# A streaming encoder layer on one Trainium2 core: the first prompt tile routed by quarters of its heads

## The reference

```python
def peer_block(xb, w_pq, sub_keys, u_tab, v_tab):
    q = (xb @ w_pq).reshape(T, PEER_HEADS, 2, D_HALF)
    s = jnp.einsum('thcd,ckd->thck', q, sub_keys)
    s1, i1 = lax.top_k(s[:, :, 0], PEER_TOPK)
    s2, i2 = lax.top_k(s[:, :, 1], PEER_TOPK)
    cand = (s1[..., :, None] + s2[..., None, :]).reshape(T, PEER_HEADS, PEER_TOPK * PEER_TOPK)
    cidx = (i1[..., :, None] * N_KEYS + i2[..., None, :]).reshape(T, PEER_HEADS, PEER_TOPK * PEER_TOPK)
    best, sel = lax.top_k(cand, PEER_TOPK)
    eidx = jnp.take_along_axis(cidx, sel, axis=-1)
    g = jax.nn.softmax(best, axis=-1)
    u = jnp.take(u_tab, eidx, axis=0)
    a = jax.nn.gelu(jnp.einsum('thkd,td->thk', u, xb).astype(jnp.float32))
    vv = jnp.take(v_tab, eidx, axis=0)
    return jnp.einsum('thk,thkd->td', (g * a).astype(xb.dtype), vv)
```

## Time and profile before

| what | value |
|---|---|
| three runs | 2685.37, 2688.01, 2691.91 us, median 2688.01 |
| the profiled execution | 2683.65 us, of which its span is 2682.1 us |
| mean granted PE clock | 0.971 |
| busy share of the span | PE 93%, PEld 83%, DVE 67%, POOL 40%, ACT 35% |
| memory traffic | 723.70 MB, mean 270 GB/s |

### The profile page before, as it was taken

The page is one execution under the profiler, slowest core; times in us unless marked ns, Lnnn a source line. Parts: engine busy times, 40 slices in busy tenths (PEclk is TensorE's granted clock), DMA queues, the critical chain, the costliest instruction groups (busy, mean ns, idle before and its releaser), DMA issues.

```text
span 2682.1 us, 41611 instructions
## 1 busy us (share of the span) xinstructions
PE 2483.2 (93%) x15886; PEld 2232.5 (83%) x15886; DVE 1793.9 (67%) x2208; ACT 941.4 (35%) x1146; POOL 1069.9 (40%) x615
## 2 busy tenths in 40 slices
PE   5989899999799999698888899999999999999998
PEld 4878777788799999698888899899888777787777
DVE  4555654543465666586756665667589889898898
ACT  3354544522323333222222222233333333333332
POOL 1020101020000037778878888842145444444442
PEclk8999999999899999899999999999999999999999
DMA  5453544495234556798889999998799999999997
GB/s 183 133 181 111 180 127 137 143 393 171 81 111 143 158 159 159 202 308 285 292 287 293 294 307 300 301 342 357 270 395 412 412 413 412 412 412 413 410 412 284
DMA packets 221593, 723.70 MB, mean 270 GB/s; under 512 B 55656, under 2 KB 105576, under 8 KB 154823
## 3 DMA queue, kind: packets, MB, share of 16 engines
q1 hardware_dynamic: 132304, 397.46, 41.6%
q0 software_dynamic: 86976, 315.74, 33.1%
q10 hardware_dynamic: 2231, 9.44, 0.9%
HBM read 680.73 MB, written 41.83 MB: 269 GB/s over the span
## 4 chain that ended last, share of the span: by engine, by line
PE 36%; POOL 22%; DMA 18%; DVE 13%; issue 7%; ACT 1%; SPq 1%; DVEq 1%; ACTq 0%; POOLq 0%
POOL g_dense L473 18%; PE banks L1208 10%; PE banks L1210 10%; PE banks L1209 10%; DMA a_tile<-a_dense 6%; DVE h L1160 5%; DMA raw<-in_v_tab 4%; POOL u_row L467 4%; DMA g_dense<-route,route_place 3%; PE banks L1434 2%; DMA v_raw<-in_v_tab 2%; DVE v_lo L1168 2%; DMA raw<-in_w_out 1%; DVE ring_lo L1168 1%; DVE ring_lo L808 1%
## 5 line engine op out<-in xcount | busy, mean ns | idle before, releaser
L1208 PE MATMUL banks<-xT_hi,ring_hi 128*128 128x256 f32 (+1 forms) x2304 | 698.9, 303 | 92.9 <-DVE ring_lo L1057 88.1
L473 POOL DMA_INDIRECT g_dense<-route,route_place x256 | 503.0, 1965 | 488.8 <-DVE route_place L1116 371.3
L1209 PE MATMUL banks<-xT_lo,ring_hi 128*128 128x256 f32 (+1 forms) x2304 | 672.1, 292 | 0.0
L1210 PE MATMUL banks<-xT_hi,ring_lo 128*128 128x256 f32 (+1 forms) x2304 | 672.0, 292 | 0.0
L1208 PEld LDWEIGHTS banks<-xT_hi,ring_hi 128*128 128x128 f32 x2304 | 448.9, 195 | 98.9 <-DVE ring_lo L1057 93.9
L501 POOL DMA_INDIRECT v_row<-in_v_tab,route_place x128 | 338.4, 2644 | 418.0 <-DVE h L1160 367.7
L1057 DVE TENSOR_TENSOR ring_lo<-banks,ring_hi 128x1024 fp32r<-128x1024 f32 x256 | 309.8, 1221 | 209.3 <-ACT ring_hi L732 208.0
L1209 PEld LDWEIGHTS banks<-xT_lo,ring_hi 128*128 128x128 f32 x2304 | 448.9, 195 | 0.0
L1210 PEld LDWEIGHTS banks<-xT_hi,ring_lo 128*128 128x128 f32 x2304 | 447.4, 194 | 0.0
L732 ACT ACTIVATE ring_hi<-banks 128x1024 fp32r<-128x1024 f32 x256 | 262.5, 1026 | 520.8 <-PE banks L1434 519.4
L1124 DVE CUSTOM_DVE_ANT_0 u_row<-u_row,x_rows 128x2048 f32<-128x2048 f32 x128 | 291.8, 2287 | 168.9 <-DMA u_row<-in_u_tab,route_place 168.0
(11 more groups left out here) (216 smaller groups left out, 3802.0 us busy)
## 6 DMA issues: line engine op xcount, KB each, us to landing
raw<-in_u_tab SPq DMA_DIRECT2D x128, 1024.0 KB, 5.9
v_raw<-in_v_tab SPq DMA_DIRECT2D x64, 1024.0 KB, 14.7
raw<-in_v_tab SPq DMA_DIRECT2D x64, 1024.0 KB, 14.3
raw<-in_w_in SPq DMA_DIRECT2D x160, 256.0 KB, 3.5
raw<-in_w_out SPq DMA_DIRECT2D x64, 256.0 KB, 4.3
g_dense<-zeros POOLq DMA_DIRECT2D x16, 1024.0 KB, 27.6
raw<-in_w_pq SPq DMA_DIRECT2D x64, 256.0 KB, 3.7
a_dense<-gelu_out SPq DMA_DIRECT2D x128, 128.0 KB, 5.9
```

The costliest lines, as they stand in the source:

```text
L473: pool.indirect_dma_start(out=places, out_offset=bass.IndirectOffsetOnAxis(ap=routeU[:, t, 2, j:j + 1], axis=0), in_=route[:, t, 0, j:j + ...
L1208: MM(out, h1, h2, start=first, stop=False)
L1209: MM(out, h1, l2, start=False, stop=False)
L1210: return MM(out, l1, h2, start=False, stop=last)
```

## The change

- Tile 0 is routed by `routing_quarter(nb, j)`: two heads at a time, in 6 parts, with buffers of its own (`cand4`, `eq4`). Quarter 0 has its parts behind steps 8, 9 and 12 of the query projection, quarter 1 behind step 13 and m = 0 to 3, quarter 2 in m = 4 to 8, quarter 3 in m = 8 to 12. Each quarter has its own exponential on ACT and its own count in `rt_ready`.
- The sample tile is routed in m = 13 to 25, tile 1 in every second m from 26 to 50. Dots are spread over m = 26 to 124, 1.306 a step.
- POOL scatters tile 0 as its quarters come. The sample rows' gathers begin at slot 104 of tile 0, one behind every two scatters; behind tile 0 POOL gathers alone, up to row 36; then it waits for tile 1 and sends two gathers with every three scatters.

```diff
-TILE_ORDER = (0, 2, 1)
-FIRST, SECOND = N_SWEEPS + N_PARTS, N_SWEEPS + 2 * N_PARTS
+QUARTERS = 4
+QUARTER_IN_PQ = {8: ((0, 0),), 9: ((0, 1), (0, 2), (0, 3)), 12: ((0, 4), (0, 5)), 13: ((1, 0), (1, 1))}
+QUARTER_IN_U = {0: ((1, 2),), 1: ((1, 3),), 2: ((1, 4),), 3: ((1, 5),), 4: ((2, 0),), 5: ((2, 1),), 6: ((2, 2), (2, 3)),
+                7: ((2, 4),), 8: ((2, 5), (3, 0)), 9: ((3, 1),), 10: ((3, 2), (3, 3)), 11: ((3, 4),), 12: ((3, 5),)}
+ROUTED = QUARTERS + NT - 1
+SAMPLES = 13
+DOTS_FROM = SAMPLES + N_PARTS
-AHEAD_ROWS = 48
+APART = 104
...
-            sp.wait_ge(rt_ready, NT)
+            sp.wait_ge(rt_ready, ROUTED)
...
-            for n in range(N_SCATTER // 2):
-                t, j = divmod(2 * n, SLOTS)
...
+            for j in range(SLOTS):
+                if j % (2 * TOPK) == 0:
+                    pool.wait_ge(rt_ready, 1 + j // (2 * TOPK))
+                if j % TOPK == 0 and j:
+                    pool.wait_ge(g_scat, 16 * j)
+                scatter(0, j)
+                if j == APART:
+                    pool.wait_ge(rt_ready, QUARTERS + 1)
+                if j >= APART and j % 2 == 0:
                     gather_dot(gathered)
                     gathered += 1
+            while gathered < dots_after(DOTS_FROM + 2 * N_PARTS) + NUB - 1:
+                gather_dot(gathered)
+                gathered += 1
+            pool.wait_ge(rt_ready, ROUTED)
+            for j in range(SLOTS):
+                if gathered < DOTS and j % 3 < 2:
+                    gather_dot(gathered)
+                    gathered += 1
+                if j % TOPK == 0:
+                    pool.wait_ge(g_scat, 16 * (SLOTS + j))
+                scatter(1, j)
...
+            few = [P, 2, TOPK, TOPK]
+
+            def routing_quarter(nb, j):
+
+                heads, places, pair = slice(2 * nb, 2 * nb + 2), slice(32 * nb, 32 * nb + 32), (2 * nb, 2 * nb + 1)
+                k = slice(0, 8) if j == 0 else slice(8, 16)
+                if j == 0:
+                    V.tensor_copy(tf[:, 4 * nb:4 * nb + 4, :], ti[:, 0, 4 * nb:4 * nb + 4, :])
+                    V.tensor_tensor(cand4[:, :, :].rearrange("p h (a b) -> p h a b", a=TOPK),
+                                    tvh[:, 0, heads, 0, :].unsqueeze(3).broadcast_to(few),
+                                    tvh[:, 0, heads, 1:2, :].broadcast_to(few), ALU.add)
+                    drain()
+                elif j == 1:
+                    for i, h in enumerate(pair):
+                        V.match_replace(cand4[:, i, :], bv[:, h, 0:8], cand4[:, i, :], NEG)
+                    drain()
+                if j < 2:
+                    for i, h in enumerate(pair):
+                        V.max(bv[:, h, k], cand4[:, i, :])
+                    drain()
+                    for i, h in enumerate(pair):
+                        V.max_index(bi[:, h, k], bv[:, h, k], cand4[:, i, :])
+                elif j == 2:
+                    V.tensor_copy(bst[:, 0, heads], bv[:, heads, 0])
+                    V.tensor_scalar(bhl[:, 0, heads], bi[:, heads, :], 4, None, ALU.logical_shift_right)
+                    V.tensor_scalar(bhl[:, 1, heads], bi[:, heads, :], 15, None, ALU.bitwise_and)
+                    drain()
+                    V.tensor_tensor(bv[:, heads, :], bv[:, heads, :], bst[:, 0, heads].unsqueeze(2).broadcast_to([P, 2, TOPK]),
+                                    ALU.subtract).then_inc(best_rdy, 1)
+                    V.tensor_copy(bhf[:, :, heads, :], bhl[:, :, heads, :])
+                elif j < 5:
+                    c = j - 3
+                    V.tensor_tensor(eq4[:, :, :, :], bhf[:, c, heads].unsqueeze(3).broadcast_to(few),
+                                    cst[:, C_IOTA:C_IOTA + 16].unsqueeze(1).unsqueeze(1).broadcast_to(few), ALU.is_equal)
+                    drain()
+                    V.tensor_tensor(eq4[:, :, :, :], eq4[:, :, :, :], tfh[:, heads, c:c + 1, :].broadcast_to(few), ALU.mult)
+                    drain()
+                    V.tensor_reduce(route[:, 0:1, 1 + c, places].rearrange("p o (h k) -> p (o h) k", h=2), eq4[:, :, :, :], AX.X, ALU.add)
+                else:
+                    dve.wait_ge(best_exp, nb + 1)
+                    V.tensor_reduce(bst[:, 0, heads], bv[:, heads, :], AX.X, ALU.add)
+                    drain()
+                    V.reciprocal(bst[:, 1, heads], bst[:, 0, heads])
+                    drain()
+                    V.tensor_tensor(route[:, 0:1, 0, places].rearrange("p o (h k) -> p (o h) k", h=2), bv[:, heads, :],
+                                    bst[:, 1, heads].unsqueeze(2).broadcast_to([P, 2, TOPK]), ALU.mult)
+                    i1 = route[:, 0:1, 1, places].rearrange("p o x -> p (o x)")
+                    i2 = route[:, 0:1, 2, places].rearrange("p o x -> p (o x)")
+                    place = bhf[:, 0, heads, :].rearrange("p h k -> p (h k)")
+                    V.scalar_tensor_tensor(out=place, in0=i2, scalar=float(P), in1=i1, op0=ALU.mult, op1=ALU.add)
+                    drain()
+                    V.tensor_scalar(routeU[:, 0:1, 2, places].rearrange("p o x -> p (o x)"), place, cst[:, C_AD + NT:C_AD + NT + 1],
+                                    cst[:, C_AD:C_AD + 1], ALU.mult, ALU.add).then_inc(rt_ready, 1)
+                drain()
+
...
+                for quarter, part in QUARTER_IN_PQ.get(s, ()):
+                    routing_quarter(quarter, part)
...
+                for quarter, part in QUARTER_IN_U.get(m, ()):
+                    routing_quarter(quarter, part)
                 if tile_part(m):
-                    n, j = tile_part(m)
-                    routing_part(TILE_ORDER[n], j)
+                    routing_part(*tile_part(m))
```

More of the change, by code:

```diff
@@ L57 @@
 UR = 4
-AHEAD_ROWS = 48
+APART = 104
 def tile_part(m):
[L63 to L66, removed]
+    if SAMPLES <= m < DOTS_FROM:
+        return NT - 1, m - SAMPLES
+    i = m - DOTS_FROM
+    return (1, i // 2) if i >= 0 and i % 2 == 0 and i < 2 * N_PARTS else None
 def dots_after(m):
-    return min(DOTS, max(m + 1 - SECOND, 0) * DOTS // (LAST_DOT - SECOND))
+    return min(DOTS, max(m + 1 - DOTS_FROM, 0) * DOTS // (LAST_DOT - DOTS_FROM))
 TD = SEQ
@@ L208, in hybrid_layer @@
         cand = at("cand", WK + 32, [P, PH, 256])
+        cand4 = at("cand_quarter", WK + 44, [P, 2, 256])
+        eq4 = at("eq_quarter", WK + 46, [P, 2, TOPK, TOPK])
         eqb = at("eq", WK + 40, [P, PH, TOPK, TOPK])
@@ L503, in gather_row @@
                     in_offset=bass.IndirectOffsetOnAxis(ap=routeU[:, NT - 1, 1, k:k + 1], axis=0)).then_inc(row_in[k % NVB], 16)
-            pool.wait_ge(rt_ready, NT)
             pool.wait_ge(dot_done, DOTS)
@@ L724, in _, with best_weights @@
                     score_evac(s // 4 - 1)
+                for quarter, part in QUARTER_IN_PQ.get(s - 1, ()):
+                    if part == 2:
+                        act.wait_ge(best_rdy, quarter + 1)
+                        A(bv[:, 2 * quarter:2 * quarter + 2, :], bv[:, 2 * quarter:2 * quarter + 2, :], ACT.Exp).then_inc(best_exp, 1)
+            def best_weights(n, heads):
+                act.wait_ge(best_rdy, n + 1)
+                A(bv[:, heads, :], bv[:, heads, :], ACT.Exp).then_inc(best_exp, 1)
             def u_hi(m, k):
@@ L749, in _ @@
                     A(adot[:, :], adot[:, :], ACT.Gelu_apprx_tanh).then_inc(dot_gelu, 1)
-                if m and tile_part(m - 1) and tile_part(m - 1)[1] == 6:
-                    act.wait_ge(best_rdy, tile_part(m - 1)[0] + 1)
-                    A(bv[:, :, :], bv[:, :, :], ACT.Exp).then_inc(best_exp, 1)
+                for quarter, part in QUARTER_IN_U.get(m - 1, ()):
+                    if part == 2:
+                        best_weights(quarter, slice(2 * quarter, 2 * quarter + 2))
+                if tile_part(m - 1) and tile_part(m - 1)[1] == 6:
+                    best_weights(QUARTERS + (NT - 1 - tile_part(m - 1)[0]), slice(0, PH))
                 gelu(m, m % 2)
@@ L1041, in sweep @@
                 drain()
[L1043 to L1058, removed]
             tvh = tv[:, :, :, :].rearrange("p t (h c) k -> p t h c k", c=2)
@@ L1101, in routing_part @@
                     route_index(t, 1, 2)
-                    dve.wait_ge(best_exp, TILE_ORDER.index(t) + 1)
+                    dve.wait_ge(best_exp, QUARTERS + NT - t)
                     V.tensor_reduce(bst[:, 0, :], bv[:, :, :], AX.X, ALU.add)
@@ new lines, in _ @@
+            for s in range(16):
+                split_lo(BASE_WPQ + s, s % 2)
+                if s == 2:
+                    V.scalar_tensor_tensor(out=xrow[:, :], in0=hh[:, NT - 1, :], scalar=rrx[:, NT - 1:NT], in1=gbc[:, :],
+                                           op0=ALU.mult, op1=ALU.mult)
+                    drain()
+                for n in SWEEPS_AT.get(s, ()):
+                    sweep(n)
+                for quarter, part in QUARTER_IN_PQ.get(s, ()):
+                    routing_quarter(quarter, part)
@@ L1120, in dot, with u_lo @@
+            def u_lo(m, k):
```

(5 more changed lines are left out.)

## The result

The changed kernel takes 2569.47 us (median of four runs, 2566.96 to 2572.26) against 2687.25 us for the kernel before (four runs, 2685.37 to 2691.91): ratio 0.956, interval 0.9543 to 0.9576. That is 118 us less. The forecast was 2592 us with 2572 to 2630 as its range, so the direction and most of the size were right, and the result lies 2.5 us under the range. The profiled execution took 2569.49 us.

What follows compares the result with a forecast made beforehand. POOL was taken to bound the u stage from 1094 to 1762 us, PE elsewhere. Losses of 8.7 + 7.6 + 2 + 8 = 26 us for 121.6 gave 2588, on the median's scale 2592 us, range 2572 to 2630.

Steps and rivals of the forecast that it cites:

- the wait of the first dot: Dot 0 in m = 26: wanted at 1047.2 us, row landed at 1055.9, so 8.7 us lost (0 to 19).
- the stretch of tile 1: 91 gathers with 128 scatters from about 1262 us: POOL keeps up, some waits come through, 8 us lost (0 to 34).
- nearly all is gained: Rival: POOL ahead at slot 104 and no waits later, loss 5 us, 2571 us; chance 0.12.
- the quarters cost PE nothing: Projection and m = 0 to 4: routing parts fit DVE's idle time, cost 0, at most 5 us over the five steps.
- every quarter is ready before POOL wants it: Tile 0's scatters: 37.3 us per 16, quarters counted at about 809.4, 876, 911 and 941 us, each ready in time.
- the gathers beside the last scatters of tile 0: 12 gathers at 6.31 us each where DVE wants one every 5.73: 7.6 us lost (3 to 13).
- the steps with two dots: Steps 32, 42 and 48 join two dots with a part of 2.3 to 3.9 us: 2 us lost.
- my two sums: POOL's cost per gather with 1.5 scatters beside tile 1: 5.25 us, or 5.5 charged per dot, both under 5.73.
- Landing becomes the bound: Rival, slower: where loads, gathers and scatters meet, landing at 20 us makes 200 us lost, 2766 us; chance 0.04.

Runs made afterwards that it cites:

- the quarters alone: The changed kernel with POOL's old order, a gather behind every two scatters from slot 48 on through both tiles: 2633.64 us, ratio 0.9801.
- the order alone: The kernel before, tile 0 routed whole in m = 5 to 17, with POOL's new loops: 2701.12 us, ratio 1.0051.
- the later start: The changed kernel, except that POOL's first scatter waits for quarter 1 too: 2628.98 us.
- the one-operand dot: The kernel before with each dot replaced by a sum over the gathered row alone: 2592.23 us, ratio 0.965.
- the plain product: The kernel before with each dot replaced by a two-operand product without the sum: 2682.41 us against 2681.74, ratio 0.9985.
- the two on how much POOL has to spare: The changed kernel with its dots ending at m = 110 instead of 124, 2629.71 us, and at m = 118, 2591.35 us.
- the last experiment: The changed kernel with a gather behind every scatter, not every second, from slot 104 of tile 0: 2558.41 us, ratio to the kernel before 0.9535.

## Why the prediction was right, and where it was not

**What failed.** The result lies 2.5 us under the range of 2572 to 2630. The mechanism held; what failed is the sum of the losses left in the u stage, 26 us forecast for 10.2 measured. Two of its terms were mis-sized: the wait of the first dot, 8.7 us forecast and 0 measured, and the stretch of tile 1, 8 forecast and 0.3 measured. The range made it worse: it was said to take in the rival "nearly all is gained", and that rival's own time, 2571, lies under its lower end of 2572.

**Right: the bound and the mechanism.** POOL bounded the stretch from 1094 us on. The five experiments on this reading (the quarters alone, the order alone, the later start, the one-operand dot and the plain product) landed inside what it gave; the two on how much POOL has to spare did not. The loss of the u stage was the right thing to count.

**Right: the quarters cost PE nothing.** The projection's window shows PE busy 107.42 of 108 us, with DVE at 83.12, and PE did not wait for a low part from m = 1 to m = 29. In the kernel before the same stretch reads:

```profile
738.00:846.00 108.00, 107.42 (x653) 107.10 (x653) 67.49 (x299) 30.90 (x33) 0.00 (x0) 1.00 0.39 127
```

But the margin was thinner than I wrote. An operation over 512 elements took 0.69 us, not the 0.57 that a quarter of 2.28 gives, and the last part of quarter 0 ended 0.1 us ahead of the next low part:

```profile
807.51 0.30 DVE L1180 TENSOR_SCALAR route_place<-best_hl_f,cst 128x32 uint32<-128x32 f32 x1
807.90 2.29 DVE L834 TENSOR_TENSOR ring_lo<-raw,ring_hi 128x2048 fp32r<-128x2048 f32 x1
```

In m = 0 to 4 I misread a row. The 884.7 us of the earlier trace rows is the end of the first half of the low part of m = 5. The second half waits for ACT and ends at 887.7, 0.3 us before PE's 888.0:

```profile
886.49 1.23 DVE L1057 TENSOR_TENSOR ring_lo<-banks,ring_hi 128x1024 fp32r<-128x1024 f32 x1 [1.79 <-ACT ring_hi L732]
```

The idle time before that second half is what took up the parts: in the changed kernel both halves run back to back (884.28 to 886.63), and nothing is lost.

**Wrong, at little cost: every quarter is ready before POOL wants it.** I gave quarter 1 8 us in hand. POOL came to slot 32 faster than I had paced it and stood idle there for 3.14 us, until quarter 1 was routed (the row at 876.00 of POOL's timeline above). The other slots at which it waits show 1.7 to 5.7 us for landing or issue, so little of the 3.14 is the quarter's own.

**Wrong: the first dot.** I took 8.7 us; it was 0. I paced 104 scatters by the three blocks of the earlier trace rows, 37.3 us per 16. They took (1035.64 - 808.72)/104 x 16 = 34.9, because five of the six waits at every sixteenth slot were 1.7 to 3.3 us instead of 4.3 to 5.7. From the first scatter to slot 104 I had 238.6 us (6 x 37.3 + 8 x 1.85) and it took 226.9. The 11.7 us so won put POOL at slot 104 ahead of the samples' routes, and from there the routes decide: dot 0 started at 1045.47 without a wait.

**Nearly right: the gathers beside the last scatters of tile 0.** About 10.2 us for 7.6: 8.7 in step 30 and some 1.5 of the 2.7 in step 33, whose second dot waited 1.39 us for its row. The larger loss comes from one wait for landing at slot 112, not from the mean deficit.

**Right in size: the steps with two dots.** I took 2 us for steps 32, 42 and 48. Step 32 cost 1.2, seen by itself in the last experiment as a late step 33; the other two cost nothing.

**Wrong: the term of the tile 1 stretch, set by caution.** I took 8 us; it was 0.3 by the gelus behind step 48. The cost per gather lay between my two sums (5.41 for 5.25 and 5.5), so the arithmetic gave 0 and I put 8 on it. Three row buffers covered it all: POOL was ahead and waited for a dot before 20 of its 84 gathers. That caution had its point, though at the wrong place: at a demand of 5.38 us for 5.73, the same stretch lost 24 us.

Summed: 26.3 us lost were forecast and 10.2 came (the last step is 1.7 us short in both kernels, which the forecast left out). Another 2.8 us fell outside the u stage; that is 18.9 of the 22.5 by which the median was missed. The rest is the step from the profiled execution to the median. I added 4.4 us, since the profiled execution of before lay under its median; that of after lies on its own.

**The rivals.** "Nearly all is gained", with a loss of 5 us and 0.12, was the closest; it deserved more, since both sums of the main stretch spoke for it. "Landing becomes the bound" has a true core: in the kernel with one-operand dots the engines reach share 1.00 at 340 GB/s. The changed kernel runs at 0.96 with 342.

**On the page.** The Trainium skill (SBUF — State Buffer, Who interferes with whom) infers that a plain two-input operation leaves descriptor writing alone. For the indirect DMAs here the plain product, with scatters at 2000 ns, says otherwise; the measurement decides. The same section of the Trainium skill also says that a DVE instruction with two inputs in SBUF contends with a GpSimd instruction that reads SBUF. The scatters and gathers here do take `route_place` as an input, so this trace agrees with that sentence. No run here tells whether the reading or the writing of descriptors is what stands still.

## What to carry to other kernels

Where one in-order engine feeds another, write down its cost per item and the consumer's time per item for every stretch, and keep them a few per cent apart: at 5.41 for 5.73 us nothing was lost; when DVE asked for one every 5.38, the cost itself rose to 5.58 and 24 us were lost. An earlier start and a cheaper item are two repairs that may be worth little or less than nothing alone (53 us, and 14 us the wrong way) and 118 together. When POOL's DMA instructions look long, see what DVE runs beside them before blaming the DMA engines.

## What the hardware showed

- A POOL instruction that issues an indirect DMA stands still while DVE runs an instruction with two operands in SBUF, custom or plain. In the kernel before, 103 of the 104 that started within a dot were over 0.3 us longer than the usual 1.55 (scatter) or 0.99 us (gather), and in the median they ended that usual time, less 0.12 us, after the dot had ended. A scatter took 2.0 us in the mean in the stretch with either kind of dot, 1.57 with a reduction of one operand of the same length. The first scatter of the changed kernel shows it by itself: it started at 808.72 within a low part of the projection, both operands in SBUF, which ran to 810.19, and ended at 811.77.
- A low part of the u stage, one operand in PSUM and one in SBUF, does not hold it up: of 101 POOL instructions of the kernel before that started within one (and not within a dot), none was over 0.15 us longer.
- The other way round nothing shows: the 128 dots of the changed kernel last 2278 to 2359 ns beside POOL's work.
- Loads, gathers and scatters together brought the DMA engines to share 1.00 at 340 GB/s, while the v stage moves 401 GB/s at the same share. The share, not the rate, tells how near the end is.
